# Query and key rows of a differential-attention layer turned once, with their second halves written across the partitions or copied

## Chip, core and metric

One Trainium2 chip, one core, one program launch. The metric is the device time of the program in microseconds (us), lower is better.

## What is computed

The layer is one block of a streaming encoder: RMS norm, differential attention, residual, RMS norm, squared-ReLU MLP, residual, all in float32, 2048 rows of 1024 columns. The part that the change touches, from the reference:

```python
q = rms_norm(q.reshape(B, S, H, 2, Dh), q_g)        # H = 8 heads, 2 maps, Dh = 64
k = rms_norm(k.reshape(B, S, H, 2, Dh), k_g)
s = jnp.einsum('bqhmd,bshmd->bhmqs', qi, k) * scale   # scores of both maps m
p = jax.nn.softmax(jnp.where(mask, s, -jnp.inf))
pd = p[:, :, 0] - lam * p[:, :, 1]
o = einsum('bhqs,bshe->bqhe', pd, v)
```

The mask is chunk-causal: row tile t (128 rows) reads the row tiles 0 to t.

## The kernel before, in words

**Arithmetic.** Every float32 factor is split into a rounded high part (written by ScalarE) and a low part (the difference, written by VectorE), and the products of the parts are added in PSUM. For the scores a map has only 64 inner positions, so the 128 partitions hold two halves. The keys' tile `k_s[:, m, rows]` holds map m's high part in partitions 0 to 63 and its low part in 64 to 127. The queries' tiles `q_hi[:, m, rows]` and `q_lo[:, m, rows]` hold the same 64 values twice, once in each half. Two matmuls per bank of 512 keys then give high times high plus high times low (L559) and low times high plus low times low (L561).

**Tiling.** The work goes over 8 heads and, in each, 16 row tiles; a step is a = 16 h + j. Step a scores row tile j of head h and, beside it, projects row tile n = a + 16, that is the same tile of the next head (`pe_project`, L401, 24 matmuls at L417), so that q, k and v of a head are ready one head ahead. A prologue does the projection of head 0 beside the first norm and the turning of the input rows (L1457, L1134, L1302, L1297). Head 7 has no projection beside it; it has the output projection and the second norm instead. The MLP follows.

**The path of q and k.** For tile n: `act_keep_qkv` (L428, ScalarE) copies the projection out of PSUM; `act_square_qk` (L434) squares it; `dve_sum_qk` (L441) sums it; `pool_factor_qk` (L447, GpSimd) takes the power; `pool_norm_qk` (L453, GpSimd) writes the normed q and k, each map twice side by side, 4 x 2 x 64 columns, into `qk_nat`; `pe_turn_qk` (L509) turns them with four 128x128 transposes into one PSUM bank of `turn`; `act_turned_qk` writes `q_hi` (L525) and the keys' high halves (L526), each one instruction of 128 x 256 on ScalarE; `dve_turned_qk` writes `q_lo` (L533, 128 x 256) and the keys' low halves (L536, 64 x 256) on VectorE. Tile n is turned one step after it was projected and scored 15 steps later.

**The order of the work.** Each engine runs a list written out by hand, with semaphores between the engines; nothing is reordered at run time. Three forms of a step follow one another:
- `first_step` (j = 0),
- `small_step` (j = 1 to 7). TensorE: scores of both maps, turning of the step before's probabilities (L634), projection, `pe_turn_qk`, values (L662, L664). ScalarE: exponentials (L601), turned probabilities (L643), norm of an output (L703), L428, L434, L465, then L525 and L526, then L674. VectorE: maxima (L576), low part of the turned probabilities (L649), combination of the maps (L617 to L623), L441, then L533 and L536, then the output (L682),
- `big_step` (j = 8 to 15). TensorE: scores of map 0, late values, first half of the projection, `pe_turn_qk`, scores of map 1, turned probabilities between the quarters of the projection, values. VectorE: two maxima of map 0 (L578), output, combination (L623) of the step before, a maximum of map 1, then L533 and L536, the second maximum of map 1, then L649. Here `turn` has two banks used in turn, and the second bank of probabilities is turned into the bank from which L536 has just read (`wait_slot`, L479).

SyncE's queue issues all large transfers in order: in the prologue, for each row tile, `x_in` (L978) and `store_u` (L973); in the steps `load_u` (L716), `store_output` (L709), weights (L377). VectorE's sums take their scratch row `sum_row` from `qk_nat` in head 7.

Of the kernel before, what the change touches and what calls it, by code (L numbers as in the profile page):

```python
# [19 lines left out]
P = 128  # L20
# [199 lines left out]
def attention_engines(nc, ctx, x, norm1_g, w_in, q_g, k_g, lambdas, w_out, sub_g, norm2_g, o_dram, u_dram,  # L220
# [37 lines left out]
    qk_nat = sb("qk_nat", [P, 4, 2, DH])  # L258
# [37 lines left out]
    sum_row = qk_nat.rearrange("p g a d -> p (g a d)")  # L296
# [13 lines left out]
    def staged(pair, o, part):  # L310
# [28 lines left out]
        sem("v_hi_set"), sem("v_lo_set"), sem("qk_normed"), sem("qk_turned"))  # L339
    q_hi_set, k_hi_set, q_lo_set, k_lo_set = (  # L340
# [108 lines left out]
    def pool_norm_qk(pool, n):  # L449
        pool.wait_ge(qk_rs_set, n + 1)  # L450
        if n:
            pool.wait_ge(qk_turned, n)
        pool.tensor_tensor(  # L453
            qk_nat[:, :, :, :],
            qkv[:, n % 2, 0:2 * HD].rearrange("p (g d) -> p g d", g=4).unsqueeze(2)
            .to_broadcast([P, 4, 2, DH]),
            qk_rs[:, :].unsqueeze(2).unsqueeze(3).to_broadcast([P, 4, 2, DH]),
            ALU.mult).then_inc(qk_normed, 1)
# [45 lines left out]
    def pe_turn_qk(pe, n):  # L504
        slot = slot_of("qk", n)
        pe.wait_ge(qk_normed, n + 1)
        wait_slot(pe, "qk", n)
        for g in range(4):
            last = pe.transpose(turn[:, slot, g * P:(g + 1) * P],  # L509
                                qk_nat[:, g, :, :].rearrange("p a d -> p (a d)"), ident[:, :])  # L510
        last.then_inc(qk_turned, 1)

    def turned(slot, g, rows=slice(0, P)):
        return turn[rows, slot, g * 2 * P:(g + 1) * 2 * P].rearrange("p (m r) -> p m r", m=2)

    def act_turned_qk(act, n):
        hp, j = split(n)  # L520
        slot, rows = slot_of("qk", n), slice(j * P, (j + 1) * P)
        act.wait_ge(qk_turned, n + 1)
        if hp:
            act.wait_ge(scored, scores_through(n - NT))
        act.activation(q_hi[:, :, rows], turned(slot, 0), ACT.Copy, scale=g_q[:, :]).then_inc(q_hi_set, 1)  # L525
        act.activation(k_s[hp % 2][:, :, rows], turned(slot, 1), ACT.Copy).then_inc(k_hi_set, 1)  # L526

    def dve_turned_qk(dve, n):
        hp, j = split(n)
        slot, rows, low = slot_of("qk", n), slice(j * P, (j + 1) * P), slice(DH, P)  # L530
        k = k_s[hp % 2]
        dve.wait_ge(k_hi_set, n + 1)
        dve.scalar_tensor_tensor(q_lo[:, :, rows], turned(slot, 0), g_q[:, :],  # L533
                                 q_hi[:, :, rows].bitcast(F32), ALU.mult, ALU.subtract)\
           .then_inc(q_lo_set, 1)
        dve.tensor_tensor(k[low, :, rows], turned(slot, 1, low), k[low, :, rows].bitcast(F32), ALU.subtract)\  # L536
           .then_inc(k_lo_set, 1)
# [428 lines left out]
    def sync(sp):  # L966
# [9 lines left out]
        for j in range(2, NT):  # L976
            sp.wait_ge(u_normed, j - 1)
            sp.dma_start(x_in[:, j % 2, :], x[j * P:(j + 1) * P, :]).then_inc(x_loaded[j % 2], 16)  # L978
            if BIG <= j < BIG + 4:
                load_weights(sp, 1, (j - BIG,))  # L980
            store_u(j - 2)
        store_u(NT - 2)
        load_u(sp, NT)
        store_u(NT - 1)
        for n in range(NT + 1, NT + 3):
            load_u(sp, n)
        for a in range(ALL):
# [56 lines left out]
    def gpsimd(pool):  # L1044
# [17 lines left out]
        pool.wait_ge(ident_set, 4)  # L1062
        x_factor(0)
# [1176 lines left out]
```

## Time and profile before

| | us |
|---|---|
| median of 3 runs | 2828.84 (2827.75 to 2829.13) |
| the profiled execution | 2827.03 |
| its span, first to last instruction | 2825.2 |
| TensorE busy | 2730.3 (97%) |
| VectorE busy | 1899.1 (67%) |
| ScalarE busy | 1504.8 (53%) |
| GpSimd busy | 1077.9 (38%) |

The prologue ends at 115 us, heads 0 to 6 with their projections take the stretch from there to about 1242 us, head 7 lasts until about 1510 us, and the MLP fills the rest. Matmuls overlap one another, so a busy TensorE can still lose time: the distance between the starts of two of them says more than their durations. Durations of the other engines are those of single instructions; on VectorE and ScalarE an instruction can begin a little before the one ahead of it has ended.

### The profile page before, as it was taken

How to read it: one execution, taken by the hardware profiler on the slowest of the kernel's cores; microseconds unless marked ns; L12 is line 12 of the kernel's file. 1: busy time of each engine (PE TensorE's matmuls, PEld its weight loads, DVE VectorE, ACT ScalarE, POOL GpSimd, SP SyncE). 2: the span in 40 equal slices, each digit the busy share in tenths (PEclk: the TensorE clock that was granted, in tenths of full speed). 3: DMA queues.
4: the chain of work that ended last, by engine and by line, in shares of the span. 5: the costliest groups of instructions: out<-in, count | busy, mean ns of one | idle time of the engine just before them, and what ended most of it. 6: DMA issues, size and time to landing. Idle time of an engine off the chain costs nothing.

```text
span 2825.2 us, 42849 instructions
## 1 busy us (share of the span) xinstructions
PE 2730.3 (97%) x14784; PEld 2368.7 (84%) x14784; DVE 1899.1 (67%) x2726; ACT 1504.8 (53%) x2987; POOL 1077.9 (38%) x956
## 2 busy tenths in 40 slices
PE   7999999999999999988999989999999999999999
PEld 7998989889898988977887778888888888888887
DVE  5777777777777777775676665555555555666655
ACT  5666666666666666654554434444444444444443
POOL 5633424243332424232001344444444444444443
PEclk9999999999999999989999999999999999999999
DMA  7742424233242523224455986666667976666663
GB/s 255 263 149 80 166 96 150 96 131 116 94 164 81 166 96 122 101 71 142 166 183 178 352 331 239 236 256 267 247 257 279 336 287 235 233 237 238 237 238 132
DMA packets 181808, 544.09 MB, mean 193 GB/s; under 512 B 14736, under 2 KB 88208, under 8 KB 136592
## 3 DMA queue, kind: packets, MB, share of 16 engines
q1 hardware_dynamic: 180608, 541.91, 52.5%
q8 instruction: 90, 1.47, 0.2%
q14 instruction: 70, 0.57, 0.1%
q10 hardware_dynamic: 1040, 0.13, 0.0%
HBM read 470.81 MB, written 71.17 MB: 192 GB/s over the span
## 4 chain that ended last, share of the span: by engine, by line
PE 70%; DVE 14%; issue 7%; ACT 4%; DMA 3%; POOL 1%; SPq 1%; ACTq 0%; DVEq 0%; POOLq 0%
PE banks L2150 21%; PE banks L2126 21%; PE banks L417 11%; DVE mx L578 5%; PE banks L662 4%; PE banks L821 3%; DVE p_all L623 3%; PE banks L634 3%; PE banks L559 2%; PE banks L561 2%; PE banks L664 1%; ACT p_all L601 1%; ACT pt_hi L643 1%; PE banks L509 1%; DVE pt_lo L649 1%
## 5 line engine op out<-in xcount | busy, mean ns | idle before, releaser
L2126 PE MATMUL banks<-u,w 128*128 128x512 f32 x2688 | 614.9, 390 | 3.3 <-issue 2.6
L417 PE MATMUL banks<-w_hi,u_ring 128*128 128x384 f32 x2048 | 590.1, 348 | 12.0 <-DVE w_lo L396 5.0
L2126 PEld LDWEIGHTS banks<-u,w 128*128 128x128 f32 x2688 | 505.3, 188 | 109.9 <-issue 3.9
L2150 PE MATMUL banks<-w,a_hi 128*128 128x512 f32 x1792 | 553.8, 390 | 7.2 <-DVE y L2048 7.2
L1891 POOL TENSOR_TENSOR w<-w_raw,w 128x1024 fp32r<-128x1024 f32 x96 | 245.3, 2570 | 560.0 <-DVE a_lo L2029 281.8
L601 ACT ACTIVATE p_all<-banks,bias 128x1024 f32<-128x1024 f32 (+7 forms) x384 | 331.2, 865 | 138.9 <-DVE bias L581 71.0
L2150 PEld LDWEIGHTS banks<-w,a_hi 128*128 128x128 f32 x1792 | 337.3, 188 | 78.0 <-issue 7.6
L417 PEld LDWEIGHTS banks<-w_hi,u_ring 128*128 128x128 f32 x2048 | 376.4, 189 | 16.6 <-issue 10.6
L2150 PE MATMUL banks<-w,a_lo 128*128 128x512 f32 x896 | 349.5, 390 | 0.0
L447 POOL TENSOR_TENSOR qk_rs<-qk_var,minus_half 128x4 f32<-128x4 f32 x128 | 129.4, 1011 | 574.2 <-DVE qk_var L441 574.2
L417 PE MATMUL banks<-w_lo,u_ring 128*128 128x384 f32 x1024 | 344.9, 337 | 0.0
L662 PE MATMUL banks<-v_s,pt_hi 128*128 128x256 f32 x1088 | 282.6, 337 | 30.6 <-DVE pt_lo L649 20.6
L649 DVE TENSOR_TENSOR pt_lo<-banks,pt_hi 128x512 fp32r<-128x512 f32 (+2 forms) x320 | 189.7, 608 | 173.3 <-ACT pt_hi L643 172.6
L2048 DVE TENSOR_TENSOR y<-banks,y 128x1024 f32<-128x1024 f32 x224 | 267.5, 1219 | 54.3 <-PE banks L2150 46.4
L1940 ACT ACTIVATE w<-w_raw 128x1024 fp32r<-128x1024 f32 x190 | 198.1, 1051 | 177.8 <-PE banks L2126 89.8
L643 ACT ACTIVATE pt_hi<-banks 128x512 fp32r<-128x512 f32 (+2 forms) x320 | 169.6, 533 | 182.2 <-PE banks L634 181.9
L559 PE MATMUL banks<-k_s,q_hi 128*128 128x512 f32 (+3 forms) x640 | 254.4, 400 | 2.8 <-ACT p_all L601 2.8
L578 DVE TENSOR_REDUCE mx<-banks 128x1 f32<-128x1024 f32 (+7 forms) x256 | 246.1, 985 | 12.2 <-PE banks L561 10.5
L662 PEld LDWEIGHTS banks<-v_s,pt_hi 128*128 128x128 f32 x1088 | 206.7, 190 | 50.1 <-issue 36.6
L664 PE MATMUL banks<-v_s,pt_lo 128*128 128x128 f32 x1088 | 243.3, 224 | 0.0
L1953 ACT ACTIVATE a_hi<-hid 128x1024 fp32r<-128x1024 f32 x96 | 101.9, 1062 | 247.2 <-PE banks L2150 176.0
L561 PE MATMUL banks<-k_s,q_lo 128*128 128x512 f32 (+3 forms) x640 | 232.3, 367 | 0.0
(151 smaller groups left out, 4726.7 us busy)
## 6 DMA issues: line engine op xcount, KB each, us to landing
u<-u_factors SPq DMA_DIRECT2D x224, 1024.0 KB, 9.5
u_ring<-u_scratch SPq DMA_DIRECT2D x112, 1024.0 KB, 5.2
w_raw<-in_mlp_w SPq DMA_DIRECT2D x128, 512.0 KB, 6.6
u_scratch<-u_ring SPq DMA_DIRECT2D x16, 1024.0 KB, 5.0
w_raw<-in_a_w_in SPq DMA_DIRECT2D x96, 128.0 KB, 4.7
u_factors<-q_hi SPq DMA_DIRECT2D x23, 512.0 KB, 4.4
u_factors<-q_lo SPq DMA_DIRECT2D x23, 512.0 KB, 4.4
p_all<-in_x SPq DMA_DIRECT2D x16, 512.0 KB, 5.7
```

The lines of the kernel that those rows point to most:

```text
L417: last = pe.matmul(proj[:, 0:3 * HD], u[:, part, kt, :], w[:, kt, :], start=(kt == 0 and part == 0 and w is w_hi), stop=(kt == KT - 1 and ...
L559: pe.matmul(scores[:, at, 0:width], q_hi[:, m, rows], k_s[h % 2][:, m, keys], start=not masked, stop=False, skip_group_check=True)
L561: last = pe.matmul(scores[:, at, 0:width], q_lo[:, m, rows], k_s[h % 2][:, m, keys], start=False, stop=True, skip_group_check=True)
L578: dve.tensor_reduce(mx[:, m, k:k + 1], piece, AX.X, ALU.max).then_inc(piece_max, 1)
L601: act.activation(dst, flat[:, place * BANK:place * BANK + keys.stop - keys.start], ACT.Exp, bias=bias[:, par, m:m + 1], accum_out=z_part[: ...
L649: dve.tensor_tensor(pt_lo[:, g % 2, 0:width], turn[:, slot_of("p", a, n), 0:width], pt_hi[:, g % 2, 0:width].bitcast(F32), ALU.subtract).t ...
L662: pe.matmul(o_acc[:, 0:2 * HD], pt_hi[:, g % 2, c * P:(c + 1) * P], v, start=(n == 0 and c == 0), stop=False, skip_group_check=True)
L664: last = pe.matmul(o_acc[:, 0:HD], pt_lo[:, g % 2, c * P:(c + 1) * P], v[:, 0:HD], start=False, stop=(n == nb - 1 and c == tiles - 1), ski ...
L1891: pool.tensor_tensor(weight(w, 1), full_weight(it, w), weight(w, 0).bitcast(F32), ALU.subtract)\
L2048: dve.tensor_tensor(part, banks[:, at:at + 2, :], part, ALU.add).then_inc(y_added, 1)
L2126: last = pe.matmul(banks[:, UP_BANKS[p] + f, :], w[:, 2 * k2 + k, f * P:(f + 1) * P], u[:, :, part, k, :], start=(STARTS[p] and k2 == 0 an ...
L2150: last = pe.matmul(banks[:, DOWN_BANKS[p] + t, :], a[:, p % 2, f, t * P:(t + 1) * P], b[:, f, :], start=(STARTS[p] and f == 0 and a is a_h ...
```

## The change

`qk_nat` holds each map once (4 x 64 columns) and lies in a row of its own that `sum_row` shares. Two transposes per tile turn q's two maps and k's two maps; map m then lies in half m of the partitions (partitions 0 to 63 or 64 to 127). ScalarE and VectorE take each of their two instructions apart into one per half, 64 x 128 each. The second copy of q's high part, in the other half, is written by two transfers on SyncE's queue (`store_other_q`), for which the scores wait. The keys' low part is written by VectorE across the halves: it reads half m and writes half 1 - m. `q_lo` is written in half m alone; the other half is set to zero once by GpSimd at the start, so that low times low is left out.

```diff
-    qk_nat = sb("qk_nat", [P, 4, 2, DH])
+    sum_row = sb("sum_row", [P, BANK])[:, :]
+    qk_nat = sum_row[:, 0:2 * HD].rearrange("p (g d) -> p g d", g=4)
...
         pool.tensor_tensor(
-            qk_nat[:, :, :, :],
-            qkv[:, n % 2, 0:2 * HD].rearrange("p (g d) -> p g d", g=4).unsqueeze(2)
-            .to_broadcast([P, 4, 2, DH]),
-            qk_rs[:, :].unsqueeze(2).unsqueeze(3).to_broadcast([P, 4, 2, DH]),
-            ALU.mult).then_inc(qk_normed, 1)
+            qk_nat, qkv[:, n % 2, 0:2 * HD].rearrange("p (g d) -> p g d", g=4),
+            qk_rs[:, :].unsqueeze(2).to_broadcast([P, 4, DH]), ALU.mult).then_inc(qk_normed, 1)
...
-        for g in range(4):
+        for g in range(2):
             last = pe.transpose(turn[:, slot, g * P:(g + 1) * P],
-                                qk_nat[:, g, :, :].rearrange("p a d -> p (a d)"), ident[:, :])
+                                qk_nat[:, 2 * g:2 * g + 2, :].rearrange("p m d -> p (m d)"), ident[:, :])
...
+    HALVES = (slice(0, DH), slice(DH, P))
+
+    def turned(slot, g, m):
+        return turn[HALVES[m], slot, g * P:(g + 1) * P]
...
-        act.activation(q_hi[:, :, rows], turned(slot, 0), ACT.Copy, scale=g_q[:, :]).then_inc(q_hi_set, 1)
-        act.activation(k_s[hp % 2][:, :, rows], turned(slot, 1), ACT.Copy).then_inc(k_hi_set, 1)
+        for m, half in enumerate(HALVES):
+            high_q = act.activation(q_hi[half, m, rows], turned(slot, 0, m), ACT.Copy, scale=g_q[half, :])
+        high_q.then_inc(q_hi_set, 1)
+        for m, half in enumerate(HALVES):
+            high_k = act.activation(k_s[hp % 2][half, m, rows], turned(slot, 1, m), ACT.Copy)
+        high_k.then_inc(k_hi_set, 1)
...
-        dve.scalar_tensor_tensor(q_lo[:, :, rows], turned(slot, 0), g_q[:, :],
-                                 q_hi[:, :, rows].bitcast(F32), ALU.mult, ALU.subtract)\
-           .then_inc(q_lo_set, 1)
-        dve.tensor_tensor(k[low, :, rows], turned(slot, 1, low), k[low, :, rows].bitcast(F32), ALU.subtract)\
-           .then_inc(k_lo_set, 1)
+        for m, half in enumerate(HALVES):
+            low_q = dve.scalar_tensor_tensor(q_lo[half, m, rows], turned(slot, 0, m), g_q[half, :],
+                                             q_hi[half, m, rows].bitcast(F32), ALU.mult, ALU.subtract)
+        low_q.then_inc(q_lo_set, 1)
+        for m, half in enumerate(HALVES):
+            low_k = dve.tensor_tensor(k[HALVES[1 - m], m, rows], turned(slot, 1, m), k[half, m, rows].bitcast(F32),
+                                      ALU.subtract)
+        low_k.then_inc(k_lo_set, 1)
+
+    def store_other_q(sp, n):
+        rows = slice(n % NT * P, (n % NT + 1) * P)
+        sp.wait_ge(q_hi_set, n + 1)
+        if n >= 2:
+            sp.wait_ge(q_doubled[n % 2], 32 * (n // 2))
+        for m, half in enumerate(HALVES):
+            sp.dma_start(q_hi[HALVES[1 - m], m, rows].bitcast(F32), q_hi[half, m, rows].bitcast(F32))\
+              .then_inc(q_doubled[n % 2], 16)
...
             pe.wait_ge(q_lo_set, a + 1)
+            pe.wait_ge(q_doubled[a % 2], 32 * (a // 2 + 1))
+            if a == 0:
+                pe.wait_ge(q_zeroed, 2)
...
             store_u(j - 2)
+            if j >= 4:
+                store_other_q(sp, j - 4)
...
+        for n in range(NT - 4, NT - 1):
+            store_other_q(sp, n)
         for a in range(ALL):
...
                 store_output(sp, a - 2)
+            if a + NT - 1 < ALL:
+                store_other_q(sp, a + NT - 1)
...
         pool.wait_ge(ident_set, 4)
+        for m in range(2):
+            pool.memset(q_lo[HALVES[1 - m], m, :].bitcast(F32), 0.0).then_inc(q_zeroed, 1)
+            pool.wait_ge(q_zeroed, m + 1)
```

## Rows read from the trace of the kernel before

**Rows 1.** The page: busy time of each engine, its share of the span, instructions.
```profile
PE 2730.3 (97%) x14784; PEld 2368.7 (84%) x14784; DVE 1899.1 (67%) x2726; ACT 1504.8 (53%) x2987; POOL 1077.9 (38%) x956
```
**Rows 2.** A stretch: length, busy of PE, PEld, DVE, ACT, POOL, granted clock, DMA.
```profile
850.00:1000.00 150.00, 146.05 (x956) 134.08 (x955) 113.68 (x222) 99.30 (x264) 56.69 (x79) 1.00 0.37 123
```
**Rows 3.** The chain that ended last, steps 10 and 11, head 3 (start, us, what).
```profile
685.67 0.39 DVE q_lo L533
...
686.09 0.43 DVE k_s L536
...
687.97 0.61 DVE pt_lo L649
...
688.71 0.35 PE banks L662
...
691.90 0.42 DVE qk_var L441
```
**Rows 4.** TensorE in order of time, small step 2, head 3 (start, us, what).
```profile
619.70 0.60 PE L509 MATMUL banks<-ident,qk_nat 128*128 128x128 f32 x4
620.05 0.36 PE L662 MATMUL banks<-v_s,pt_hi 128*128 128x256 f32 x1
```
**Rows 5.** VectorE by shape, 402 to 1150 us (busy us, mean ns, idle before, releaser).
```profile
L649 DVE TENSOR_TENSOR pt_lo<-banks,pt_hi 128x128 fp32r<-128x128 f32 x19 | 5.5, 292 | 8.9 <-ACT pt_hi L643 8.9
...
L533 DVE SCALAR_TENSOR_TENSOR q_lo<-banks,g_q,q_hi 128x256 fp32r<-128x256 f32 x74 | 35.6, 481 | 16.2 <-ACT k_s L526 15.7
...
L536 DVE TENSOR_TENSOR k_s<-banks,k_s 64x256 fp32r<-64x256 f32 x74 | 31.6, 428 | 2.3
...
L682 DVE SCALAR_TENSOR_TENSOR o_sum<-banks,rz,o_tmp 128x128 f32<-128x128 f32 x75 | 26.3, 350 | 6.9 <-ACT o_tmp L674 5.7
```
**Rows 6.** VectorE in order of time, big step 12, head 3.
```profile
708.96 1.22 DVE L578 TENSOR_REDUCE mx<-banks 128x1 f32<-128x1024 f32 x1
710.10 0.48 DVE L533 SCALAR_TENSOR_TENSOR q_lo<-banks,g_q,q_hi 128x256 fp32r<-128x256 f32 x1
710.61 0.43 DVE L536 TENSOR_TENSOR k_s<-banks,k_s 64x256 fp32r<-64x256 f32 x1
```
**Rows 7.** ScalarE by shape, 402 to 1150 us.
```profile
L428 ACT ACTIVATE rows<-banks 128x384 f32<-128x384 f32 x75 | 36.6, 488 | 13.5 <-PE banks L417 12.4
...
L674 ACT ACTIVATE o_tmp<-banks,rz 128x128 f32<-128x128 f32 x75 | 27.6, 368 | 44.2 <-PE banks L664 44.2
...
L643 ACT ACTIVATE pt_hi<-banks 128x128 fp32r<-128x128 f32 x19 | 5.3, 277 | 2.0 <-PE banks L634 2.0
```
**Rows 8.** ScalarE in order of time, small step 2, head 3.
```profile
615.16 0.45 ACT L525 ACTIVATE q_hi<-banks,g_q 128x256 fp32r<-128x256 f32 x1
615.51 0.37 ACT L526 ACTIVATE k_s<-banks 128x256 fp32r<-128x256 f32 x1
```
**Rows 9.** VectorE in order of time, small steps 2 and 4, head 3.
```profile
618.97 0.42 DVE L649 TENSOR_TENSOR pt_lo<-banks,pt_hi 128x256 fp32r<-128x256 f32 x1 [0.31 <-ACT pt_hi L643]
...
631.77 0.69 DVE L649 TENSOR_TENSOR pt_lo<-banks,pt_hi 128x512 fp32r<-128x512 f32 x1 [0.47 <-ACT pt_hi L643]
```
**Rows 10.** TensorE in order of time, small step 4, head 3.
```profile
633.49 0.36 PE L662 MATMUL banks<-v_s,pt_hi 128*128 128x256 f32 x1
```
**Rows 11.** GpSimd in order of time: before VectorE's first work, and in the prologue.
```profile
9.28 0.19 POOL L1054 TENSOR_TENSOR x_var<-x_ss,eps 128x1 f32<-128x1 f32 x1 [7.71 <-ACT p_all L1126]
...
71.22 1.04 POOL L453 TENSOR_TENSOR qk_nat<-rows,qk_rs 128x512 f32<-128x512 f32 x1
```
**Rows 12.** VectorE in order of time: row tiles 1 and 10 normed in the prologue.
```profile
12.23 1.28 DVE L1297 SCALAR_TENSOR_TENSOR p_all<-p_all,x_rs 128x1024 f32<-128x1024 f32 x1 [0.71 <-POOL x_rs L1059]
...
71.29 2.05 DVE L1297 SCALAR_TENSOR_TENSOR p_all<-p_all,x_rs 128x1024 f32<-128x1024 f32 x1 [1.13 <-POOL x_rs L1059]
```
**Rows 13.** SyncE's queue in order of time, prologue: row tile 11's load.
```profile
69.38 0.43 SPq L978 DMA_DIRECT2D p_all<-in_x  x1
```
**Rows 14.** ScalarE in order of time, prologue: row tile 11 squared.
```profile
75.42 1.06 ACT L1126 ACTIVATE p_all<-p_all 128x1024 f32<-128x1024 f32 x1
```

More of the change, by code:

```diff
@@ L295, in attention_engines @@
     full = rows[:, 0:D].rearrange("p (n c) -> p n c", n=2)
-    sum_row = qk_nat.rearrange("p g a d -> p (g a d)")
     p_stage = at("p_stage", [P, 3, S], F32R, 128)
@@ L339, in attention_engines @@
         sem("v_hi_set"), sem("v_lo_set"), sem("qk_normed"), sem("qk_turned"))
+    q_doubled, q_zeroed = [sem("q_doubled0"), sem("q_doubled1")], sem("q_zeroed")
     q_hi_set, k_hi_set, q_lo_set, k_lo_set = (
@@ L507, in pe_turn_qk @@
         wait_slot(pe, "qk", n)
-        for g in range(4):
+        for g in range(2):
             last = pe.transpose(turn[:, slot, g * P:(g + 1) * P],
-                                qk_nat[:, g, :, :].rearrange("p a d -> p (a d)"), ident[:, :])
+                                qk_nat[:, 2 * g:2 * g + 2, :].rearrange("p m d -> p (m d)"), ident[:, :])
         last.then_inc(qk_turned, 1)
-    def turned(slot, g, rows=slice(0, P)):
-        return turn[rows, slot, g * 2 * P:(g + 1) * 2 * P].rearrange("p (m r) -> p m r", m=2)
+    HALVES = (slice(0, DH), slice(DH, P))
+    def turned(slot, g, m):
+        return turn[HALVES[m], slot, g * P:(g + 1) * P]
     def act_turned_qk(act, n):
@@ L524, in act_turned_qk @@
             act.wait_ge(scored, scores_through(n - NT))
-        act.activation(q_hi[:, :, rows], turned(slot, 0), ACT.Copy, scale=g_q[:, :]).then_inc(q_hi_set, 1)
-        act.activation(k_s[hp % 2][:, :, rows], turned(slot, 1), ACT.Copy).then_inc(k_hi_set, 1)
+        for m, half in enumerate(HALVES):
[4 more added lines that the diff above has]
+        high_k.then_inc(k_hi_set, 1)
     def dve_turned_qk(dve, n):
         hp, j = split(n)
-        slot, rows, low = slot_of("qk", n), slice(j * P, (j + 1) * P), slice(DH, P)
+        slot, rows = slot_of("qk", n), slice(j * P, (j + 1) * P)
         k = k_s[hp % 2]
         dve.wait_ge(k_hi_set, n + 1)
-        dve.scalar_tensor_tensor(q_lo[:, :, rows], turned(slot, 0), g_q[:, :],
-                                 q_hi[:, :, rows].bitcast(F32), ALU.mult, ALU.subtract)\
-           .then_inc(q_lo_set, 1)
-        dve.tensor_tensor(k[low, :, rows], turned(slot, 1, low), k[low, :, rows].bitcast(F32), ALU.subtract)\
-           .then_inc(k_lo_set, 1)
+        for m, half in enumerate(HALVES):
[14 more added lines that the diff above has]
+              .then_inc(q_doubled[n % 2], 16)
     def pe_scores(pe, a, m):
```

## The prediction, made before the change was run

> **What bounds the kernel now.** I read the page first: TensorE is busy 97% of the span, VectorE 67%, ScalarE 53% [rows 1]. That invites the answer "TensorE, so fewer transposes are time saved". The stretch view of one head says the same, 146 of 150 us, at the full granted clock of 1.00, the 2.4 GHz level [rows 2]. But busy time of matmuls overlaps, and these are means over steps with different limits, so I went to the chain of waits inside a head. In steps 10 and 11 of head 3 it doesn't follow TensorE: it runs through VectorE from the sum of squares (L441) over the maxima, the combination, q_lo (L533), k_s (L536), a maximum and pt_lo (L649), then for about 2 us through TensorE's values (L662) and the transposes of the probabilities, through ScalarE, and back to L441 [rows 3]. The transposes L509 aren't in it, and L533 and L536 are. Steps 13 to 15 look alike; in step 12 both paths arrive together. So in steps 10 to 15 the time of a step is the length of this loop. In steps 1 to 9 TensorE sets the pace, but with little to spare, as shown below.
>
> **What the change removes.** Two transposes of four per tile. The four take 0.35 us from the first one's start to the next matmul's, 0.60 us to their own end [rows 4], so two are worth 0.18 to 0.30 us. I take 0.2, as the distance of starts is what a full queue pays. Over the 112 tiles of heads 0 to 6 that is 22 us if TensorE sets the pace everywhere. GpSimd's norm writes half as much: 1.04 us becomes 0.5 to 1.04 us, estimated at 0.6. In the heads nobody waits for it, since the tile is turned a step later.
>
> **What it adds on VectorE.** Each of two instructions becomes two of 128 columns. Columns count here and partitions don't: L536 with 64 partitions takes 428 ns, though it reads 256 columns as L533 does (481). The nearest rows for 128 columns out of PSUM are L682 (350 ns, same operation as q_lo) and L649 (292 ns, same as k_s) [rows 5]. To that comes the join. L578 lasts 1.22 us and L533 starts 1.14 us after it, 0.08 of overlap; L533 lasts 0.48 and L536 starts 0.51 after it, 0.03 of gap [rows 6]. The join is dear where the partitions change. In the new code they change at each piece but the first. From the start of q_lo to whatever follows k_s: now 0.51 + 0.46 = 0.97 us; then 2 x 0.35 + 2 x 0.29 + 4 x 0.03 = 1.41 us. So **+0.44 us** per tile. If the pieces overlapped by 0.08 like full ones, 2 x 0.27 + 2 x 0.21 = 0.96: nothing added; that is the lower end. The upper end is two L533 and two L536 at their present length, +0.97.
>
> The row shows a join without overlap between L533 and L536. The Trainium skill ("VectorE: DVE Perf Modes", section on two Vector instructions with no wait between them) says why: an instruction is held until all earlier ones have finished if its input or output starts in another group of 32 partitions than the last one's. By it the second q_lo, both k_s and the instruction after them are held, which gives the same +0.44; if it did not hold, the sum would be that of the lower end.
>
> **What it adds on ScalarE.** q_hi lasts 0.45 us and its successor starts 0.35 after it, so 0.10 overlap [rows 8]. For 128 columns, L674 (scaled by a column, out of PSUM) lasts 0.37 and L643 (plain) 0.28 [rows 7]. From q_hi's start to the end of k_s: now 0.35 + 0.37 = 0.72; then 0.27 + 0.27 + 0.18 + 0.28 = 1.00. So **+0.27 us**. Ends: 0, and +0.57 if none of the three joins overlaps.
>
> **Steps 10 to 15.** VectorE's part lies in the loop whole, ScalarE's doesn't (it idles between q_hi and the next turned probabilities), and the shorter transposes aren't in it. 6 x 0.44 = 2.6 us longer per head. The second bank of probabilities is turned into the bank that L536 frees, so TensorE would stall there too.
>
> **Steps 1 to 7.** Here ScalarE and VectorE work in a ring: L428, L434, L465, q_hi, k_s high, then q_lo (it waits for ScalarE's k_s, 16.2 us in all [rows 5]), k_s low, output, maxima, exponentials, L649, the norm, L428 again. The ring grows by 0.27 + 0.44 = 0.71 us a step, 5.0 us in seven. It gives way first where ScalarE waits for TensorE before L428: 12.4 us over 75 tiles [rows 7], 4.7 heads, so 2.6 us per head; 2.4 us of lateness stay. Then TensorE's values wait for pt_lo: in step 2 pt_lo ends at 619.39 and the values start at 620.05, room 0.66 [rows 4, 9]; in step 4 632.46 against 633.49, room 1.03 [rows 9, 10]. In the later steps the room still grows a little. 2.4 less 1.0 to 1.4 leaves TensorE about 1.2 us late at the end of step 7, where the transposes alone would have made it 1.4 us early. I take **+1.2** (ends -1.4 and +3). Steps 8 and 9: the ring's lateness meets VectorE's list before the loop closes; between -0.4 (two pairs of transposes) and +0.9 (two additions of 0.44), taken at +0.3.
>
> **Step 0 and head 7.** In step 0 L509 comes after what the chain waits for; nothing either way. Head 7 turns no tile after its first step.
>
> **Prologue.** The norm of a row tile (L1297) takes 1.28 us alone and 2.05 us while GpSimd writes qk_nat beside it [rows 11, 12]. With the shorter write it loses about 0.4 us, 14 times: -6. Against it: ScalarE's 0.27 us stand ahead of the squaring of the next rows, and SyncE's queue has two more issues of 0.43 us per tile and a wait for q_hi ahead of the load of x. That load is issued at 69.38 and its rows are squared at 75.42 [rows 13, 14], hardly later than a transfer needs, so about 0.8 us for 12 tiles would show in the worst case: +10. I take 0. The Trainium skill ("GPSIMD Engine Reference") says that GpSimd shares its SBUF interfaces with VectorE where VectorE reads two SBUF inputs; the 2.05 against 1.28 us agree, and by that rule alone the prologue would gain the 6 us.
>
> **Costed at nothing.** The zeros: GpSimd is idle for 7.71 us until 9.28 [rows 11]; at its rate for 512 columns in 1.04 us two rows of 2048 take 8.3 us at most, so 0 to +0.6, once. The transfers in the heads: what is written in step a is read 15 steps later, and what stands behind them on the queue (the load of u, three steps ahead, and a store) has that room. Without this cover each tile would cost a transfer's landing.
>
> **Sum.** 7 x (2.6 + 1.2 + 0.3) + 0 = 28.7 us. On the profiled execution's 2827.0 us this is 2855.7; the median shown is 1.8 above that execution, so I forecast **2857 us**.
>
> **Rivals.**
> - *TensorE everywhere.* The 97% [rows 1] speak for it, the chain [rows 3] against. 22 us less in the heads, 3 in the prologue: 2804. Chance 0.07.
> - *The pieces overlap.* VectorE adds nothing, ScalarE 0.27. The ring's 0.27 a step fit into the waits and the room, so steps 1 to 9 gain 9 x 0.2, the loop of steps 10 to 15 stays: 7 x -1.8 = -13, 2816. For it: full-height pieces do overlap [rows 6]. Against it: the join to L536. Chance 0.10.
> - *The two cancel.* Steps 1 to 9 gain their 1.8 us, steps 10 to 15 lose 2.6, the prologue's norm gives 6 back: about 0, 2829. This needs the ring to have more room than I found. Chance 0.07.
> - *Dearer still*, one mechanism: ScalarE loses its overlap at the half changes too, so that the ring grows by 1.0 instead of 0.7 a step: 7 x 7 x 0.3 = 15 more, 2872. It decides from +0.4 us on at q_hi and k_s. Chance 0.08.
> - *Forecast*: 0.68.
>
> **Range and chances.** It leaves out the first two rivals and the last one's upper part: 2826 to 2869. A measurement of this kernel tells some 0.2%, 5.7 us, from no change. Faster by more: 0.07 + 0.10 = 0.17. Within: 0.07. Slower by more: 0.68 + 0.08 = 0.76.
>
> **What would show it.** q_lo near 350 ns and k_s near 290 ns, with starts 0.38 and 0.32 apart; steps 10 to 15 longer by 0.4 us each; TensorE's idle time ahead of L662, released by L649, up from steps 2 on; ScalarE's idle time ahead of L428 gone; L1297 at about 1.6 us; no wait of TensorE for a transfer. I'm wrong if the pieces start under 0.3 us apart, or if steps 1 to 7 come out shorter.

## The result: 2% slower, twice what was forecast

| | before | after |
|---|---|---|
| median | 2828.39 us (4 runs, 2827.75 to 2829.13) | 2890.42 us (4 runs, 2889.58 to 2891.30) |
| profiled execution | 2827.03 us | 2889.86 us |
| its span | 2825.2 us | 2888.1 us |

The ratio is 1.022 (95% interval 1.0208 to 1.0232): 62 us more, where the prediction had 28.7. The direction was right, and 2890 lies above the upper end of the range, 2869.

**Profile after.** The page's part 1, and the first line of its part 4 (shares of the chain that ended last, by engine):

```profile
PE 2733.2 (95%) x14528; PEld 2336.3 (81%) x14528; DVE 1937.4 (67%) x2982; ACT 1577.5 (55%) x3243; POOL 1028.7 (36%) x958
...
PE 50%; DVE 22%; issue 12%; ACT 11%; DMA 3%; POOL 1%; SPq 1%; ACTq 0%; DVEq 0%; POOLq 0%
```

TensorE executes 256 instructions fewer than in [rows 1] (two transposes for each of 128 tiles) and its share has gone from 97% to 95%: there is more time in which it stands still. In lines of the changed kernel (q_hi is L526, k_s high L529, q_lo L538, k_s low L542, the kept values L429, pt_lo L669, scores L579, exponential L621), VectorE and ScalarE by shape from 402 to 1150 us; columns as in [rows 5]:

```profile
L538 DVE SCALAR_TENSOR_TENSOR q_lo<-banks,g_q,q_hi 64x128 fp32r<-64x128 f32 x136 | 47.4, 349 | 36.6 <-ACT k_s L529 35.1
L542 DVE TENSOR_TENSOR k_s<-banks,k_s 64x128 fp32r<-64x128 f32 x137 | 39.6, 289 | 3.1
...
L526 ACT ACTIVATE q_hi<-banks,g_q 64x128 fp32r<-64x128 f32 x136 | 48.5, 357 | 1.5 <-PE banks L507 0.6
L529 ACT ACTIVATE k_s<-banks 64x128 fp32r<-64x128 f32 x136 | 36.9, 271 | 2.4
L429 ACT ACTIVATE rows<-banks 128x384 f32<-128x384 f32 x69 | 33.7, 489 | 0.0
```

The durations are as predicted (349 and 289 ns; L682 and L649 of [rows 5] were the right neighbours). ScalarE's idle time ahead of the kept values, 12.4 us in [rows 7], is gone. And q_lo now waits 35.1 us for ScalarE where it waited 15.7 [rows 5]: that is the first sign of what the prediction missed. One tile in order of time, small step 2 of head 3 (the tile of [rows 8]), ScalarE and then VectorE; "x2" is a pair of pieces, with the time from the first's start to the second's end:

```profile
640.73 0.72 ACT L526 ACTIVATE q_hi<-banks,g_q 64x128 fp32r<-64x128 f32 x2
641.48 0.55 ACT L529 ACTIVATE k_s<-banks 64x128 fp32r<-64x128 f32 x2
642.06 0.37 ACT L694 ACTIVATE o_tmp<-banks,rz 128x128 f32<-128x128 f32 x1
...
642.07 0.71 DVE L538 SCALAR_TENSOR_TENSOR q_lo<-banks,g_q,q_hi 64x128 fp32r<-64x128 f32 x2 [0.98 <-ACT k_s L529]
642.82 0.59 DVE L542 TENSOR_TENSOR k_s<-banks,k_s 64x128 fp32r<-64x128 f32 x2
643.44 0.35 DVE L702 SCALAR_TENSOR_TENSOR o_sum<-banks,rz,o_tmp 128x128 f32<-128x128 f32 x1
```

ScalarE's pair of q_hi takes 0.72 = 2 x 0.36: no overlap at all. k_s starts 0.75 after q_hi's first piece. Over all 128 tiles the medians of the distances of starts are 0.36, 0.39, 0.28 us, and 0.30 us to the successor; k_s is finished 1.30 us after q_hi's start, where it was 0.73: **+0.57 us**. On VectorE they are 0.36, 0.39, 0.30 and 0.32 us, together 1.37 instead of 0.97: **+0.39 us** (0.395 before rounding).

**Where the 62.8 us of span went.** I measured each step as the distance from its first q_lo score matmul to that of the next step. Head 3, after less before:

| step 0 | 1 | 2 | 3 | 4 | 5 | 6 | 7 | 8 | 9 | 10 | 11 | 12 to 15 |
|---|---|---|---|---|---|---|---|---|---|---|---|---|
| -0.23 | +0.57 | +0.76 | +0.68 | +0.35 | +0.34 | +0.10 | +0.23 | **+2.45** | +0.66 | +0.61 | +0.47 | +0.39 each |

One head is 8.6 us longer (162.0 to 170.6), heads 0 to 6 together 60.2, the prologue 0.7 us shorter, head 7 with the rest 3.3 us longer. Steps 10 to 15 are +2.64 (predicted +2.6). Steps 1 to 9 are **+6.16** (predicted 1.2 + 0.3 = +1.5), and 7 x 4.7 = 33 us is nearly the whole miss of 34. A single step stands out, step 8. TensorE's waits, 402 to 1150 us, after (total us, times, longest us):

```profile
PE banks L682 <- DVE pt_lo L669: 18.5, 44, 0.7
PE banks L654 <- DVE k_s L542: 10.4, 32, 0.4
PE banks L579 <- ACT p_all L621: 8.1, 9, 1.5
```

The first line was 6.0 us in 18 times, the second wasn't there, the third was 2.0 us in 5 times with 0.4 the longest. The third one is step 8. The kernel before, in order of time, ScalarE and TensorE in step 8 of head 3; the first line is the matmul at which the step begins:

```profile
659.68 0.40 PE L561 MATMUL banks<-k_s,q_lo 128*128 128x512 f32 x1
...
662.28 1.12 ACT L601 ACTIVATE p_all<-banks,bias 128x1024 f32<-128x1024 f32 x1 [1.11 <-DVE bias L581]
...
663.43 0.28 PE L561 MATMUL banks<-k_s,q_lo 128*128 128x128 f32 x1
...
663.54 0.50 PE L559 MATMUL banks<-k_s,q_hi 128*128 128x512 f32 x1
```

and the changed kernel at the same place:

```profile
687.40 0.39 PE L581 MATMUL banks<-k_s,q_lo 128*128 128x512 f32 x1
...
690.94 0.28 PE L581 MATMUL banks<-k_s,q_lo 128*128 128x128 f32 x1
...
691.50 1.11 ACT L621 ACTIVATE p_all<-banks,bias 128x1024 f32<-128x1024 f32 x1 [1.11 <-DVE bias L601]
...
692.76 0.50 PE L579 MATMUL banks<-k_s,q_hi 128*128 128x512 f32 x1 [1.55 <-ACT p_all L621]
```

In steps 8 and up the first map's scores and the second's share PSUM banks, so map 1's first wide matmul must wait for map 0's first exponential to have read them. Before, the exponential ended at 663.40 and the matmul started at 663.54, hardly later than TensorE got there. There was no room. After, TensorE is through at 691.2 and stands for 1.55 us. The exponential itself waited for the maximum (1.11 us), and that for VectorE's list: it is the lateness of ScalarE's and VectorE's ring that arrives here. From the step's first matmul the exponential starts after 4.10 us instead of 2.60, so it comes 1.50 us late; the step is 2.45 us longer, and the other 0.95 come behind it, where TensorE also waits for k_s (0.23 us) and pt_lo (0.41 us).

### The profile page after: what moved, and what is told of

The parts are those of the page before. It is cut to its first block, busy times and chain, and to the rows that moved or that the text cites. A ratio compares the mean times of both kernels' runs of the same rounds, so it can differ in the third digit from the quotient of the medians.

```text
span 2888.1 us, 43360 instructions
## 1 busy us (share of the span) xinstructions
PE 2733.2 (95%) x14528; PEld 2336.3 (81%) x14528; DVE 1937.4 (67%) x2982; ACT 1577.5 (55%) x3243; POOL 1028.7 (36%) x958
## 4 chain that ended last, share of the span: by engine, by line
PE 50%; DVE 22%; issue 12%; ACT 11%; DMA 3%; POOL 1%; SPq 1%; ACTq 0%; DVEq 0%; POOLq 0%
PE banks L2179 21%; PE banks L2155 20%; DVE mx L598 7%; ACT p_all L621 4%; DVE p_all L643 3%; PE banks L682 3%; PE banks L841 2%; DVE k_s L542 2%; DVE q_lo L538 2%; PE banks L418 2%; DVE bias L596 2%; ACT pt_hi L663 2%; ACT k_s L529 1%; ACT q_hi L526 1%; DVE pt_lo L669 1%
## 5 line engine op out<-in xcount | busy, mean ns | idle before, releaser
L621 ACT ACTIVATE p_all<-banks,bias 128x1024 f32<-128x1024 f32 (+7 forms) x384 | 330.9, 864 | 142.6 <-DVE bias L601 69.3
L682 PE MATMUL banks<-v_s,pt_hi 128*128 128x256 f32 x1088 | 283.8, 338 | 53.1 <-DVE pt_lo L669 43.2
L669 DVE TENSOR_TENSOR pt_lo<-banks,pt_hi 128x512 fp32r<-128x512 f32 (+2 forms) x320 | 189.1, 607 | 174.6 <-ACT pt_hi L663 174.4
L682 PEld LDWEIGHTS banks<-v_s,pt_hi 128*128 128x128 f32 x1088 | 206.6, 190 | 82.1 <-issue 68.5
L579 PE MATMUL banks<-k_s,q_hi 128*128 128x512 f32 (+3 forms) x640 | 256.1, 403 | 13.6 <-ACT p_all L621 13.5
```

What stands on the lines that cost most here:

```text
L579: pe.matmul(scores[:, at, 0:width], q_hi[:, m, rows], k_s[h % 2][:, m, keys], start=not masked, stop=False, skip_group_check=True)
L621: act.activation(dst, flat[:, place * BANK:place * BANK + keys.stop - keys.start], ACT.Exp, bias=bias[:, par, m:m + 1], accum_out=z_part[: ...
L682: pe.matmul(o_acc[:, 0:2 * HD], pt_hi[:, g % 2, c * P:(c + 1) * P], v, start=(n == 0 and c == 0), stop=False, skip_group_check=True)
```

## The experiments

The theory: (a) both engines lose the overlap of two instructions where the half changes, ScalarE included; (b) the growth of the ring counts in steps 1 to 9, not 1 to 7, and step 8 has no room. The rivals: small instructions cost their whole length wherever they stand; the transfers; TensorE still setting the pace. "Growth" is always q_hi's start to k_s's end on ScalarE plus q_lo's start to the successor on VectorE.

### VectorE's part alone

```diff
 # the kernel before, VectorE only; q_lo's other half is zeroed as in the change; semaphore increments left out
-        dve.scalar_tensor_tensor(q_lo[:, :, rows], turned(slot, 0), g_q[:, :], ...)
-        dve.tensor_tensor(k[low, :, rows], turned(slot, 1, low), k[low, :, rows].bitcast(F32), ALU.subtract)
+        for m, half in enumerate(HALVES):
+            low_q = dve.scalar_tensor_tensor(q_lo[half, m, rows], turned(slot, 0, half)[:, m, :], ...)
+        for m, half in enumerate(HALVES):
+            low_k = dve.tensor_tensor(k[HALVES[1 - m], m, rows], turned(slot, 1, half)[:, m, :], ...)
```

> The kernel before with VectorE's part of the change alone: q_lo and k_s low in two instructions each, written half by half as in the changed kernel (the product of the low parts is left out, as there); four transposes, ScalarE and no transfers as before. Theory (VectorE loses its overlap where the partitions change): from q_lo's start to the successor of k_s 1.37 us instead of 0.97, so +0.40 in each of steps 10 to 15, 2.4 us per head; in steps 1 to 7 the ring grows by 7 x 0.40 = 2.8 us, of which ScalarE's 2.6 us of waiting before it keeps the values of TensorE give all but 0.2 back, so steps 1 to 9 stay within +0.5 us per head: 2846 to 2850 us. Had steps 8 and 9 in the changed kernel their 3.1 us from VectorE's split, they would show 2 us or more here too: 2860 us. If TensorE set the pace everywhere: 2828 us.

2858.35 us against 2828.77 (ratio 1.0104, 1.0087 to 1.0121): 8 us above the expectation. Growth 0.39. Steps 10 to 15 of head 3: +2.36, as expected. Steps 1 to 7: +0.10. Steps 8 and 9: +1.31, more than the +0.5 expected and less than the 2 us and more of the alternative: the growth reaches step 8 even where ScalarE's waits swallow it on the way. That is 7 x 0.9 = 6 us of the 8. The profiled execution, at 2862.89 us the longest of the four, has another 1.56 us in step 0 of five heads, which is the granted clock and is told in the last section; how much of it the median has isn't known.

### ScalarE in as many pieces, at full height

```diff
 # the kernel before; semaphore increments left out
-        act.activation(q_hi[:, :, rows], turned(slot, 0), ACT.Copy, scale=g_q[:, :])
-        act.activation(k_s[hp % 2][:, :, rows], turned(slot, 1), ACT.Copy)
+        for m in range(2):
+            high_q = act.activation(q_hi[:, m, rows], turned(slot, 0)[:, m, :], ACT.Copy, scale=g_q[:, :])
+        for m in range(2):
+            high_k = act.activation(k_s[hp % 2][:, m, rows], turned(slot, 1)[:, m, :], ACT.Copy)
```

> The kernel before with ScalarE's q_hi and k_s each cut into two instructions by map, at the full 128 partitions: as many instructions as in the changed kernel, but no change of half. Theory (only a change of half costs the overlap of about 0.09 us): starts about 0.27, 0.27, 0.18 us apart, from q_hi's start to the end of k_s +0.27 us; in the ring 7 x 0.27 = 1.9 us per head, less than the 2.6 us of waiting there: 2828 to 2834 us. Rival (each instruction of 128 columns costs its whole length wherever it stands): starts 0.36, 0.36, 0.27 us apart, +0.55 us, 1.3 us per head over what the waits give back, and as much again where map 1's scores wait for the exponential of step 8: 2838 to 2846 us.

2834.37 us (1.0017, 1.0008 to 1.0027). ScalarE in order of time, small step 2 of head 3:

```profile
619.12 0.60 ACT L526 ACTIVATE q_hi<-banks,g_q 128x128 fp32r<-128x128 f32 x2
619.62 0.44 ACT L529 ACTIVATE k_s<-banks 128x128 fp32r<-128x128 f32 x2
619.93 0.38 ACT L678 ACTIVATE o_tmp<-banks,rz 128x128 f32<-128x128 f32 x1
```

Each of these instructions lasts as long as those of the changed kernel (0.36 and 0.28 us), but a pair takes 0.60 instead of 0.72, and the successor of all four starts 0.81 us after the first instead of 1.33. The starts are 0.25, 0.25 and 0.16 us apart. So the number of instructions isn't what costs: their overlap, 0.10 to 0.13 us each, is kept as long as the half doesn't change. Growth 0.21. Steps 1 to 7: 0.00; steps 8 and 9: +0.58, where I had expected nothing; steps 10 to 15: 0.00. Taken with the run before, the loop of steps 10 to 15 answers to VectorE and not to a growth of 0.21 on ScalarE, and step 8 to either engine.

### One change of half instead of three

```diff
 # the changed kernel
         for m, half in enumerate(HALVES):
             high_q = act.activation(q_hi[half, m, rows], turned(slot, 0, m), ACT.Copy, scale=g_q[half, :])
-        high_q.then_inc(q_hi_set, 1)
-        for m, half in enumerate(HALVES):
             high_k = act.activation(k_s[hp % 2][half, m, rows], turned(slot, 1, m), ACT.Copy)
+        high_q.then_inc(q_hi_set, 1)
```

> The changed kernel with ScalarE's four instructions in the order q of map 0, k of map 0, q of map 1, k of map 1: one change of half inside the tile instead of three. Theory (the change of half costs the overlap): the distances of starts become about 0.27, 0.28 and 0.27 us, the four end 0.2 us sooner, the ring is 7 x 0.2 = 1.4 us per head shorter, and the wait of TensorE for the exponential in step 8 (1.55 us in head 3) shrinks by about as much: 7 x 1.4 = 10 us less, 2880 us. Rival (each small instruction costs its whole length, whatever its half): no difference, 2890 us.

2872.63 us, 17.8 less than the changed kernel: the same four instructions, in another order. ScalarE, small step 2 of head 3:

```profile
632.06 0.35 ACT L526 ACTIVATE q_hi<-banks,g_q 64x128 fp32r<-64x128 f32 x1
632.31 0.26 ACT L527 ACTIVATE k_s<-banks 64x128 fp32r<-64x128 f32 x1
632.58 0.36 ACT L526 ACTIVATE q_hi<-banks,g_q 64x128 fp32r<-64x128 f32 x1
632.85 0.26 ACT L527 ACTIVATE k_s<-banks 64x128 fp32r<-64x128 f32 x1
633.14 0.37 ACT L693 ACTIVATE o_tmp<-banks,rz 128x128 f32<-128x128 f32 x1
```

Within a half k_s starts 0.25 to 0.27 after a q_hi of 0.35; at the change of half q_hi starts 0.27 after a k_s of 0.26, and L693, which starts at the first half again, 0.29 after one of 0.26. This separates (a) from its rival inside one tile. The growth is 0.71 instead of 0.96, and steps 1 to 9 give +3.85 instead of +6.16: 2.3 us less for 0.25 us less. I had reckoned with seven steps for it, and it moved the time as if in nine.

### ScalarE's part undone

```diff
 # the changed kernel; semaphore increments left out
-        for m, half in enumerate(HALVES):
-            high_q = act.activation(q_hi[half, m, rows], turned(slot, 0, m), ACT.Copy, scale=g_q[half, :])
-        for m, half in enumerate(HALVES):
-            high_k = act.activation(k_s[hp % 2][half, m, rows], turned(slot, 1, m), ACT.Copy)
+        act.activation(q_hi[:, :, rows], turn[:, slot, 0:P].unsqueeze(1).to_broadcast([P, 2, P]), ...)
+        act.activation(k_s[hp % 2][:, :, rows], turn[:, slot, P:2 * P].unsqueeze(1).to_broadcast([P, 2, P]), ...)
```

> The changed kernel with ScalarE's part undone alone: q_hi and k_s in one instruction each over all 128 partitions, each written to both maps' places (the places of the other half are overwritten as before, by the transfers and by VectorE's low part). From q_hi's start to the successor of k_s 0.62 us instead of 1.33. Theory (the growth of the ring counts in 9 steps, 1 to 9, less the 2.6 us that ScalarE's waits give back): with VectorE's 0.39 alone 9 x 0.39 - 2.6 = 0.9 us and less by what the transposes give, plus 2.4 us in steps 10 to 15: 7 x 2.4 to 7 x 3.3 us over the kernel before, 2845 to 2852 us; so ScalarE's part is worth 38 to 45 us of the 62. Rival (my prediction's sizes: ScalarE's part fits mostly into waits and room): at most 7 x 7 x 0.3 = 15 us less than now, 2875 us.

2854.62 us, a little above the 2845 to 2852 expected, and 35.8 less than the changed kernel, so ScalarE's part is well over half of the 62. Head 3: steps 1 to 9 +1.28 instead of +6.16, 4.9 us for 0.57 us of growth, a factor of 8.6; steps 10 to 15 +2.32. The steps one by one show where the saved transposes went: 4 to 7 are each 0.19 to 0.22 us *shorter* than before, and step 8 is 1.69 longer. TensorE hurries ahead and then stands for the exponential (its waits, 402 to 1150 us, as above):

```profile
PE banks L577 <- ACT p_all L619: 7.3, 9, 1.4
```

### Step 8 alone

```diff
 # the kernel before
+            if j == BIG:
+                act.wait_ge(bias_set, 2 * a + 1)
+                for i in range(2):
+                    act.activation(spare[:, i], ident[:, :].unsqueeze(1).to_broadcast([P, 2, P]), ACT.Copy)
             for k in range(np):
                 act_exp(act, a, 0, k)
```

> The kernel before with two spare copies of 128 x 256 on ScalarE between the maximum's arrival and the first exponential of step 8, once per head: the exponential comes some 0.6 us later, nothing else is changed. Theory (in step 8 TensorE's scores of map 1 wait for this exponential without room: it ends at 663.40 and they start at 663.54 in head 3): steps 8 and 9 together grow by about as much, 0.5 to 0.6 us per head, 4 to 5 us in all, 2832 us. Rival (the room of 1.0 us and more with which the prediction reckoned): 0, 2828 us.

2833.50 us (1.0014, 1.0005 to 1.0024). The exponential starts 0.63 us later from the maximum than before, and:

```profile
663.58 0.72 ACT L1232 ACTIVATE spare<-ident 128x256 bf16<-128x256 f32 x2 [1.11 <-DVE bias L582]
...
664.21 1.09 ACT L602 ACTIVATE p_all<-banks,bias 128x1024 f32<-128x1024 f32 x1
...
665.45 0.51 PE L560 MATMUL banks<-k_s,q_hi 128*128 128x512 f32 x1 [0.44 <-ACT p_all L602]
```

Step 8 is 0.60 us longer, in every head, and no other step of head 3 moves by more than 0.01. So there is no room there, which is the second half of (b). The first half rests on the tables of the section on the prediction.

### Two more transposes

```diff
 # the changed kernel, and in the same words the last version below
+        for g in range(2):
+            last = pe.transpose(turn[:, slot, (2 + g) * P:(3 + g) * P], ...)
         last.then_inc(qk_turned, 1)
```

> The changed kernel with two more transposes per tile, of the same rows into the free half of the same bank (nobody reads them). Theory: in steps 1 to 9 the ring of ScalarE and VectorE sets the pace and in steps 10 to 15 VectorE's loop, so the two transposes that were saved are worth nothing now; the turned rows only come about 0.2 us later to ScalarE, which mostly isn't waiting for them: 0 to +3 us, 2890 to 2893 us. Rival (TensorE still sets the pace in steps 1 to 9): 7 x 9 x 0.2 = +13 us, 2903 us. TensorE everywhere: +22 us, 2912 us.

2891.25 us. Steps 1 to 9 of head 3 give +6.16, the same as without them, and steps 10 to 15 +2.65 for +2.64: the saved pair is worth nothing there. Only step 0 gets longer, by 0.23 us: what it saved in the changed kernel. In the version without any change of half (below) it is otherwise:

> The last version (no change of half, transfers put later) with two more transposes per tile, as in the run with four turns on the changed kernel. Theory: here TensorE sets the pace in steps 0 to 9, so each pair of transposes costs its 0.2 us there and nothing in steps 10 to 15, which VectorE's loop sets: 7 x 10 x 0.2 = 14 us more, 2807 us. Rival (they are worth nothing, as in the changed kernel): 2793 us. Rival (worth 0.2 us everywhere): 2815 us.

2807.76 us, 14.9 more than without them (2792.87): steps 1 to 9 lose 1.52 us and step 0 another 0.22, steps 10 to 15 0.08. So 0.2 us is the right price of a pair, but only where TensorE sets the pace, and that is in eight steps (0, 2 to 7 and 9), not in the ten expected: steps 1 and 8 don't move. The time came out at the 2807 us expected all the same, as the prologue is 1.1 us longer here and executions of one kernel differ by some us.

### Without the transfers

```diff
 # the changed kernel
-                store_other_q(sp, j - 4)
-            store_other_q(sp, n)
-                store_other_q(sp, a + NT - 1)
...
+            pool.memset(q_hi[HALVES[1 - m], m, :].bitcast(F32), 0.0).then_inc(q_zeroed, 1)
```

The scores' wait for the transfers goes too, and GpSimd zeroes the other halves of q_hi as well, twice the zeros of the changed kernel.

> The changed kernel without the two transfers per tile: the second copy of q's high part isn't written (that half stays zero, so the product of q_hi with the low part of k is left out). Theory: the transfers lie beside other work; 2890 us, within 3 us. Rival (transfers and SyncE's issues delay the loads of u or the stores, or their writes slow an engine down): some us less in each head, 2870 us or below.

2889.64 us; every step of head 3 within 0.02 us of the changed kernel. The transfers cost nothing, as predicted, and twice the zeros cost nothing either.

### A version without changes of half

Both gains can be had at once. After one transpose, each of ScalarE's instructions reads the 128 turned rows and writes them to both maps' places, wrong halves included; VectorE makes the low parts from one of the two places at full height, q's once for both maps; then transfers overwrite the wrong halves.

```diff
 # the changed kernel; what these lines replace, waits and semaphores are left out
+        act.activation(q_hi[:, :, rows], turned(slot, 0).unsqueeze(1).to_broadcast([P, 2, P]), ...)
+        act.activation(k_s[hp % 2][:, :, rows], turned(slot, 1).unsqueeze(1).to_broadcast([P, 2, P]), ...)
...
+        dve.scalar_tensor_tensor(q_lo[:, 0, rows], turned(slot, 0), g_q[:, :], q_hi[:, 0, rows].bitcast(F32), ...)
+        dve.tensor_tensor(k_low[:, n % 2, :], turned(slot, 1), k_s[hp % 2][:, 0, rows].bitcast(F32), ALU.subtract)
...
+            sp.dma_start(q_hi[other, m, rows], q_hi[half, m, rows])
+            sp.dma_start(k_s[hp % 2][other, m, rows], k_low[half, n % 2, :])
```

> A version meant to beat both: two transposes per tile as in the changed kernel, but no engine's instruction starts at another half. ScalarE writes both maps' rows to both maps' places in one instruction each (128 x 256 as before), VectorE makes the low parts of both maps in one instruction of 128 x 128 each; the low part of q stands once for both maps, so that beside q_lo*k_hi the products of the other map's low q with the low k are added where the own ones were; the low part of k goes to its half by two transfers, the high part of q by two. Theory: VectorE from q_lo to the successor of k_s about 0.55 to 0.65 us instead of 0.97, so steps 10 to 15 are 0.3 to 0.4 us shorter each (-2.1 per head), steps 1 to 9 gain the two transposes (9 x 0.2 = 1.8 us): 7 x -3.9 = -27, 2800 us. Rival (transfers, four issues per tile on SyncE, delay the loads or the scores): 2828 us or more. Rival (TensorE's two transposes are worth nothing): 2813 us.

2802.60 us (0.9912, 0.9895 to 0.9929). The heads are better than expected (157.1 us instead of 162.0, head 3), but the prologue is 9.0 us longer, with these waits (20 to 115 us):

```profile
DVE p_all L1320 <- POOL x_rs L1082: 39.3, 14, 4.5
...
ACT p_all L1149 <- DMA p_all<-in_x: 25.5, 11, 3.0
```

Before, the last of these was 2.0 us in 3 times. SyncE's queue holds the load of x behind transfers that wait for VectorE's low parts of the tile. One tile later, and ahead of the store of u:

```diff
+            if j >= 5:
+                move_halves(sp, j - 5)
             store_u(j - 2)
-            if j >= 4:
-                move_halves(sp, j - 4)
```

> The version that beat both, with the transfers of the prologue put one tile later on SyncE's queue and ahead of the store of u, so that they are ready when their turn comes and no longer stand in front of the load of x. There the prologue was 9.1 us longer than before and ScalarE waited 25.5 us for x. Theory: most of it comes back, 6 to 9 us: 2794 to 2797 us. Rival (it is the traffic of the transfers that delays x, not the order on the queue): 2802 us.

**2792.87 us, 0.9873 of before (0.9856 to 0.9889)**, a prologue of 114.7 us as before. Steps 0 and 2 to 9 are 0.19 to 0.23 us shorter each, 10 to 15 about 0.5 (-3.03 together). The page's part 1, and VectorE in order of time, big step 12 of head 3:

```profile
PE 2700.3 (97%) x14528; PEld 2343.5 (84%) x14528; DVE 1839.5 (66%) x2726; ACT 1500.7 (54%) x2987; POOL 1024.1 (37%) x956
```

```profile
690.18 1.22 DVE L594 TENSOR_REDUCE mx<-banks 128x1 f32<-128x1024 f32 x1
691.31 0.34 DVE L535 SCALAR_TENSOR_TENSOR q_lo<-banks,g_q,q_hi 128x128 fp32r<-128x128 f32 x1
691.57 0.28 DVE L539 TENSOR_TENSOR k_low<-banks,k_s 128x128 fp32r<-128x128 f32 x1
691.77 0.81 DVE L594 TENSOR_REDUCE mx<-banks 128x1 f32<-128x640 f32 x1
```

Instructions as long as those of the change, but each starts 0.08 before the end of the one in front: 0.26 + 0.20 = 0.46 us for both, against 0.97 before and 1.37 after the change. The 0.51 us saved are what the steps 10 to 15 got shorter by.

## Why the prediction was right in sign and half in size

Growth of the ring against what steps 1 to 9 of head 3 cost, over all runs:

| run | ScalarE | VectorE | growth | steps 1 to 7 | 8 and 9 | 1 to 9 | 9 x growth - 2.6 |
|---|---|---|---|---|---|---|---|
| ScalarE by map | 0.21 | 0 | 0.21 | 0.00 | 0.58 | 0.58 | (-0.7) |
| VectorE alone | 0 | 0.39 | 0.39 | 0.10 | 1.31 | 1.41 | 0.9 |
| ScalarE's part undone | 0 | 0.39 | 0.39 | -0.52 | 1.80 | 1.28 | 0.9 |
| one change of half | 0.32 | 0.39 | 0.71 | 1.25 | 2.60 | 3.85 | 3.8 |
| the change | 0.57 | 0.39 | 0.96 | 3.04 | 3.12 | 6.16 | 6.0 |

The first two runs turn with four transposes, the other three with two. And step 8 by itself, in head 3; "late" is how much later than in the kernel before its first exponential starts, from the step's first q_lo matmul:

| run | late | growth | late + growth | step 8 |
|---|---|---|---|---|
| ScalarE by map | 0.21 | 0.21 | 0.42 | 0.42 |
| VectorE alone | 0.59 | 0.39 | 0.98 | 0.98 |
| ScalarE's part undone | 1.30 | 0.39 | 1.69 | 1.69 |
| one change of half | 1.47 | 0.71 | 2.18 | 2.17 |
| the change | 1.50 | 0.96 | 2.46 | 2.45 |
| step 8 alone | 0.62 | 0 | 0.62 | 0.60 |

- **What bounds the kernel**: right. The loop of steps 10 to 15 answered to VectorE, 0.39 us for 0.39, and 0.5 for 0.51 in the other direction; the transposes were worth nothing there.
- **VectorE, +0.44**: right; +0.39, no join overlaps.
- **Steps 10 to 15, +2.6**: right in the mechanism, and in the number partly by luck. VectorE's 0.39 alone gives +2.36 in its own run; the other 0.3 us of the +2.64 are in steps 10 and 11 and go when ScalarE's part is undone (+2.32) or has one change of half (+2.32). The prediction had ScalarE's part at nothing here, and its 0.44 for VectorE made up for it.
- **ScalarE, +0.27**: the first step that failed. It measured +0.57, exactly the upper end that the prediction gave "if none of the three joins overlaps". I had seen in [rows 8] that ScalarE overlaps at full height and let it keep that overlap at the changes of half, though I took it from VectorE for the same reason. Its own rival, *dearer still*, had the mechanism, but priced it in seven steps only.
- **Steps 1 to 7, +1.2**: its form was 7 x growth - 2.6 - about 1.2 of room. With the measured growth, 0.96 for 0.71, it would have given 2.9, and 3.04 came; with the 0.71 of the run with one change of half it gives 1.2, and 1.25 came. The mechanism was right, and its terms fit as far as these seven steps go; the size of the growth was off, which is 1.8 us per head.
- **Steps 8 and 9, +0.3**: the second step that failed, and the dearer with 2.8 us per head. The prediction had the ring's lateness "meet VectorE's list before the loop closes" and bounded it by 0.9. But the room of steps 1 to 7 only kept TensorE from being late itself; the ring stayed late. In step 8 TensorE waits, with no room, for something that the ring sets, so this lateness is charged there. It isn't all that the ring grew by: of 7 x 0.96 = 6.7 us, ScalarE's waits took 2.5 and TensorE's own delay 3.0, and 1.2 is left, the room that the prediction had counted as free; the exponential of step 8 comes 1.50 us late. Behind it step 8 adds one growth of its own. The second table has this sum for every run, to 0.02 us. That also says why small growths are dear here: in the run by map ScalarE's waits make each tile's growth good before the next, the exponential is 0.21 to 0.22 us late in each of steps 1 to 8, and only step 8 has no room for it. In the first table the sum over steps 1 to 9 follows 9 x growth - 2.6 for the larger growths (a line found from these runs, not forecast). Why step 9 adds 0.1 to 0.7 more stays open.
- **Step 0, 0**: a small miss. Six of the heads are 0.23 us shorter there, the price of a saved pair of transposes.
- **Together**: 1.8 + 2.8 = 4.6 us per head, times seven 32 us, of 34 missed. Left are head 7 and what follows, +3.3 us where 0 stood (1.05 in step 1 of head 7, 1.3 in its step 4, 1.4 from its step 15 to the MLP's first matmul), which I have not explained; all runs in which q and k are written in another way show 1.8 to 3.6 there, the quickest one too (+2.0).
- **Prologue, 0**: right (-0.7), though its parts are only half accounted for. The queue's term didn't show: ScalarE waited 1.5 us for x, 2.0 before. The norm of a row tile came to 1.63 us, as forecast, while GpSimd's write fell to 0.61 us:

```profile
40.46 1.63 DVE L1326 SCALAR_TENSOR_TENSOR p_all<-p_all,x_rs 128x1024 f32<-128x1024 f32 x1 [0.73 <-POOL x_rs L1085]
```

  against 2.05 in [rows 12]. All the norms of the prologue together took 25.0 us instead of 30.6, so 5.6 us would have been gained by that alone. They weren't: GpSimd's wait for the squaring of x rose from 9.7 to 15.5 us. ScalarE coming to it later is part of it at most: with ScalarE's part undone the wait is 13.0 us and the prologue 1.9 us shorter than before, so where the rest went stays open. The Trainium skill ("GPSIMD Engine Reference", section "Specifications") has the two engines share their SBUF interfaces, with contention where VectorE's instruction has two SBUF inputs, as this norm has; the 1.63 us beside a write of 0.61, 2.05 beside one of 1.04 and 1.28 alone agree.
- **Transfers and zeros at nothing**: right, shown by the run without the transfers, which has twice the zeros.
- **TensorE everywhere, the pieces overlap, the two cancel**: fell. A saved pair of transposes is worth its 0.2 us in eight steps of sixteen in the version without changes of half, and in step 0 alone in the changed kernel.

The rule that carried VectorE's part, the Trainium skill's ("VectorE: DVE Perf Modes", the section on two Vector instructions with no wait between them), agrees with every run here: 0.36 us from one q_lo of 0.34 to the next across a change of half, and 0.27 from a q_lo of 0.35 to its successor where both start at the same partition.

## What to carry over

Lateness that room has covered isn't gone: follow it to the next place where the covering engine waits for the late ones, and look at the room *there*, by the end of the wait's releaser against the start of the waiter. Splitting an instruction was cheap here (0.21 us of growth for two splits, some 6 us in all); splitting it so that each piece starts at another group of partitions is dear, on ScalarE as on VectorE, and so an order that changes the start once instead of three times gave 18 us here, a full-height layout with transfers 98 us against the change. And a pair of instructions saved on the busiest engine is worth only what the steps say in which that engine sets the pace.

## What the runs showed of the hardware

**ScalarE loses the overlap too.** At full height one activation out of PSUM starts 0.10 to 0.13 us before the end of the last; where output and input start at another half, it starts 0.01 to 0.03 us after the end, and the same holds on the way back to full height from the upper half (L529 of 0.27, L694 0.30 after it). Input and output changed together in all of these, so which of the two is enough stays open. The Trainium skill ("ScalarE: Activation LUTs", section "What ACT_TABLE_LOAD costs") gives about 93 ns of overlap for activations back to back, without this condition; by it alone ScalarE's growth would be near the 0.21 us of the run by map, and the trace of the change shows 0.57.

**The granted clock can fall in step 0.** In the run with VectorE's part alone, step 0 of heads 1 to 5 takes 16.47 us instead of 14.91. Stretches of head 3 (columns as in [rows 2]):

```profile
612.00:616.00 4.00, 2.62 (x21) 2.15 (x20) 2.40 (x8) 2.18 (x8) 4.00 (x4) 1.00 0.47 186
616.00:620.00 4.00, 3.94 (x18) 3.61 (x17) 0.99 (x2) 0.60 (x1) 1.83 (x3) 0.59 0.00 0
620.00:624.00 4.00, 4.00 (x34) 4.00 (x33) 1.52 (x5) 1.25 (x3) 0.00 (x0) 0.99 0.27 51
```

After a stretch in which TensorE is busy for only 2.62 of 4 us, the granted clock is 0.59 over the next four: most of that time is at the 1.2 GHz level, and 1.56 us are lost. In the kernel before, TensorE's gap at this place is as large (2.63 of 4 us) and the clock stays at 1.00; within one run, with ScalarE's part undone, head 2 keeps it and head 3 loses it after the same 2.62 and 2.63 us. It came in 5, 2, 1, 1 and 1 of heads 1 to 6 in five of the profiled executions (VectorE alone, ScalarE by map, ScalarE's part undone, step 8 alone, four transposes on the changed kernel). In the first of these it is 7.8 us; that execution was 4.5 us above the median of its run. In head 7, which has no projection, the clock is down at this place in every run, the kernel before included (0.56 over four us). What decides it stays open.
